# First mixers of a two-block transformer: order of decays, masks and their exponentials against splits of weights, and of a unit of v against the second decay sums

## What is computed

```python
def hgrn2(q, f_logit, i_in, lb):               # 4 heads of 64
    q = silu(q)
    f = lb + (1.0 - lb) * sigmoid(z)
    log_f = log(maximum(f, TINY))
    k = (1.0 - lb) * sigmoid(-z)
    v = i_in
    # in chunks: c = cumsum(log_f)
    #   o = (q * exp(c)) @ state + (sum_k q k exp(c_t - c_s), causal) @ v
    #   state = exp(c_last) * state + (k * exp(c_last - c)).T @ v

def forgetting_attention(q, k, v, f_logit, g_q, g_k):   # 8 heads of 64
    q = rms(q) * g_q; k = rms(k) * g_k
    dcum = cumsum(log_sigmoid(f_logit))
    logits = q @ k.T * scale + dcum_q - dcum_k          # causal softmax, @ v

for l in range(DEPTH):
    z = rms_norm(x, norm_mix[l]) @ w_in[l]
    (a_q, a_k, a_v, a_f, c_x, c_b, c_c, r_q, r_f, r_i, r_g) = split(z)
    y = concatenate([forgetting_attention(...), short_conv(...), hgrn2(...)])
    x = x + (rms(y per head) * gain, last part * silu(r_g)) @ w_out[l]
    x = x + (swiglu or the routed experts)(rms_norm(x))
# then the second block: three attentions and a squared-relu feed-forward, per layer
```

## Time and profile before

| | us |
|---|---|
| median of three runs | 2675.93 |
| lowest and highest | 2669.7, 2685.15 |
| the profiled execution, its own time | 2669.63 |
| its span | 2667.8 |
| TensorE busy | 2534.3 (95%) |
| VectorE busy | 1919.3 (72%) |
| ScalarE busy | 1489.4 (56%) |
| mean granted clock of TensorE | 0.979 |

### The profile page before, as it was taken

One profiled execution on the slowest core, in us unless ns is written; L12 is line 12 of the kernel. 1 busy time (PEld: TensorE's weight loads), 2 busy tenths in 40 slices (PEclk: granted clock), 3 DMA queues, 4 the chain that ended last, 5 costly groups with the idle time before them and its releaser, 6 DMA issues.

```text
span 2667.8 us, 38535 instructions
## 1 busy us (share of the span) xinstructions
PE 2534.3 (95%) x16700; PEld 2259.1 (85%) x16700; DVE 1919.3 (72%) x1702; ACT 1489.4 (56%) x1460; POOL 0.2 (0%) x4
## 2 busy tenths in 40 slices
PE   7989999988999999999999999899999999999998
PEld 6879999777787878787787877888999998899998
DVE  6666556665788888888888888746776575667655
ACT  5354345443676777676677767446544354465433
POOL 0000000000000000000000000000000000000000
PEclk9999999898999999999999999999999999999999
DMA  6225544221799989999998999432435443243452
GB/s 235 94 79 196 184 178 155 106 75 57 274 362 350 364 345 359 352 352 355 352 360 343 352 355 364 179 123 99 142 129 203 177 164 134 97 142 143 174 189 81
DMA packets 83451, 585.31 MB, mean 219 GB/s; under 512 B 9416, under 2 KB 11176, under 8 KB 12752
## 3 DMA queue, kind: packets, MB, share of 16 engines
q1 hardware_dynamic: 83280, 582.81, 58.8%
HBM read 581.72 MB, written 1.05 MB: 218 GB/s over the span
## 4 chain that ended last, share of the span: by engine, by line
PE 79%; DVE 12%; ACT 6%; issue 2%; DMA 1%; DVEq 0%; ACTq 0%
PE PS L1620 77%; DVE wlo L962 4%; ACT whi L526 3%; DMA raw<-in_wm 1%; PE PS L2096 1%; ACT pb L629 1%; ACT pt L643 1%; DVE hT L1011 1%; PE PS L1825 1%; DVE rstd L1003 1%; DVE pb L1130 0%; DVE stat L1118 0%; DVE pb L1112 0%; ACT hhi L553 0%; DVE hlo L978 0%
## 5 line engine op out<-in xcount | busy, mean ns | idle before, releaser
L962 DVE TENSOR_TENSOR wlo<-raw,whi 128x2048 fp32r<-128x2048 f32 x550 | 1258.1, 2290 | 409.1 <-ACT whi L526 399.4
L526 ACT ACTIVATE whi<-raw 128x2048 fp32r<-128x2048 f32 x550 | 1051.3, 1913 | 310.5 <-PE PS L1620 283.5
L1620 PE MATMUL PS<-hhi,whi 128*128 128x256 f32 x1984 | 573.4, 289 | 10.4 <-DVE wlo L962 3.8
L1620 PE MATMUL PS<-hlo,whi 128*128 128x256 f32 x1984 | 565.7, 285 | 0.0
L1620 PE MATMUL PS<-hhi,wlo 128*128 128x256 f32 x1984 | 565.5, 285 | 0.0
L1620 PEld LDWEIGHTS PS<-hhi,whi 128*128 128x128 f32 x1984 | 385.1, 194 | 25.4 <-issue 13.3
L1620 PEld LDWEIGHTS PS<-hlo,whi 128*128 128x128 f32 x1984 | 385.2, 194 | 0.2
L1620 PEld LDWEIGHTS PS<-hhi,wlo 128*128 128x128 f32 x1984 | 384.8, 194 | 0.0
L1620 PE MATMUL PS<-whi,xghi 128*128 128x512 f32 x896 | 360.5, 402 | 2.3 <-ACT pm L770 2.1
L1620 PE MATMUL PS<-wlo,xghi 128*128 128x512 f32 x896 | 355.7, 397 | 0.0
L1620 PE MATMUL PS<-whi,xglo 128*128 128x512 f32 x896 | 355.5, 397 | 0.0
(11 more groups left out here) (351 smaller groups left out, 3643.2 us busy)
## 6 DMA issues: line engine op xcount, KB each, us to landing
raw<-in_wm SPq DMA_DIRECT2D x336, 1024.0 KB, 5.5
raw<-in_ws SPq DMA_DIRECT2D x214, 1024.0 KB, 4.8
xT<-in_xT SPq DMA_DIRECT2D x4, 256.0 KB, 6.7
bsum<-in_bsum SPq DMA_DIRECT2D x1, 1024.0 KB
out_T<-hT SPq DMA_DIRECT2D x4, 256.0 KB, 2.5
lmask<-in_lmask SPq DMA_DIRECT2D x1, 512.0 KB
lbw<-in_lbw SPq DMA_DIRECT2D x1, 256.0 KB
tri<-in_tri SPq DMA_DIRECT2D x1, 256.0 KB
```

Of the source, the lines that this page charges most:

```text
L526: act.activation(whi[s % SPLIT][:], raw[s % RAW][:], ACT.Copy).then_inc(hi_ready, 1)
L962: dve.tensor_tensor(wlo[s % SPLIT][:], raw[s % RAW][:], whi[s % SPLIT][:].bitcast(F32), ALU.subtract).then_inc(lo_ready, 1)
L1620: return pe.matmul(out, a, b, start=start, stop=stop, skip_group_check=True)
```

## The change

In the lists of the three engines some entries change places; the instructions stay the same in kind and number. On VectorE the split ahead of L1212 is taken out there and the splits behind it keep their order and take other places: the splits are then unit 4 after L1212, unit 5 after `decayed(0)` and the bias, 6 after levels 0 to 2, 7 after levels 3 to 5, 8 after levels 6 and 7, 9 ahead of `decayed(1)`, 10 after `head_inverse` and levels 0 and 1. `head_inverse` comes ahead of levels 0 and 1 of the second half. On ScalarE the split of unit 5 with the copy of unit 3 comes after `cum_exp`, and the split of unit 9 with the copy of unit 7 ahead of the second `cum_exp`. On TensorE unit 7 comes ahead of `decay_sums(1)` and unit 8 ahead of levels 0 and 1 of the second half.

```diff
@@ first_mixer on ScalarE @@
                 out_of(6, flat(ri))
-                out_of(7, pair(qkT, 0))
                 after(rk_turned)
                 act.activation(flat(rk), PS[:, 4, :], ACT.Copy).then_inc(rk_ready, 1)
                 cum_exp()
+                out_of(7, pair(qkT, 0))
...
                 head_square(qkT[:], hT[:])
+                out_of(7, vtok[:, :, 0:UC], wide=NT)
                 cum_exp()
-                out_of(7, vtok[:, :, 0:UC], wide=NT)
                 head_root(5, 16, 1.0 / HD)
@@ first_mixer on VectorE @@
                 dve.tensor_tensor(flat(rq), flat(rq), flat(cy), ALU.mult)
-                drain()
                 after(f_logged, 2)
                 dve.tensor_tensor(lf[:], lf[:], lf2[:], ALU.add).then_inc(decays_ready, 1)
                 drain()
...
                 drain()
                 levels(0, (3, 4, 5))
+                drain()
                 after(decay_taken, 2)
...
                 step(dve.tensor_scalar(qs1[:], vec1(l, "qg"), HD ** -0.5, None, ALU.mult))
+                levels(0, (6, 7))
                 drain()
-                levels(0, (6, 7))
                 dve.wait_ge(decayed_ready, C.now(decayed_ready))
                 step(dve.tensor_copy(kx[:], ke[:, :, LEVELS - 1, :]))
+                drain()
                 decayed(1)
-                drain()
+                head_inverse(16)
                 levels(1, (0, 1))
-                head_inverse(16)
                 drain()
@@ first_mixer on TensorE @@
                 levels(0, (6, 7))
+                project(unit_tok, 7)
                 decay_sums(1)
-                project(unit_tok, 7)
                 head_sums(8, lambda t: selw[:, t, :], 16, hT, 5)
+                project(unit_tok, 6)
                 levels(1, (0, 1))
-                project(unit_tok, 6)
                 head_spread(8, lambda t: selT[:, t, :], 16, [4, 5])
```

## The result

The changed kernel takes 2657.89 us (median of five runs, 2656.56 to 2662.63), the kernel before 2675.93: ratio 0.9932, 95% interval 0.9909 to 0.9954. The forecast was 2665.4 us, in a range of 2651 to 2680. The gain is 18 us where the sum gave 10.5. The profiled execution took 2662.63 us (span 2660.8), the slowest of the five; that of before, 2669.63, was its fastest. So the pair of profiles differs by 7 us and the medians by 18, and the question was where the other 11 are.

What follows compares the result with a forecast made beforehand. TensorE, busy 95% of the span, was taken as the bound. Layer gains of 4.30 and 1.99 plus clock 3.19 and 5.82 made 15.3, less 4.8 gave 10.5 us: 2665.4 against the median 2675.93, range 2651 to 2680.

Steps and rivals of the forecast that it cites:

- Keys: TensorE ahead of turning the keys: the decay sum is ready earlier, so holes of 2.71 and 3.44 us go.
- The place of the first q's copy: ScalarE, copy moved behind the exponential: the exponential waits for TensorE either way, so it changes nothing.
- Split of unit 5 behind the masks: TensorE ahead of level 2: the 3.38 us hole shrinks to 0.34, gaining 3.04 in layer 0, none in layer 1.
- The unit of v ahead of the decay sums: TensorE ahead of the second decay sums: the unit covers the 1.89 us wait, gaining 1.89 in each layer.
- what is late next: TensorE ahead of the third head-norm spread: VectorE's queue makes a 3.84 us stall instead of 0.50, losing 3.34 per layer.
- The clock: TensorE's low clock in both mixers: 9.01 us could come back, less 4.8 for new stalls and logits.
- (a): Rival, chance 0.20: the clock stays high after the new stall and in the logits; all 15.3 us gained, 2660.6.
- (f): Rival, chance 0.10: only idle holes lower the clock, logits cost nothing, each new stall one short stretch; 12.1 us gained, 2663.8.
- (b): Rival, chance 0.15: the low clock stretches are long, four of 3.09 us; 2.9 us gained, 2673.0.
- (e): Rival, chance 0.05: second-half exponential serial, 7.0 us moving into each third-spread stall; slower, 2679.4, or 2685.6 with more low clock.
- (c): Rival, chance 0.06: unit 5 comes late since its split stands behind the multiplications; 6.5 us left, 2669.4.
- (d): Rival, chance 0.04: nothing shows, since another wait fills the holes ahead of the keys; 2676.

Runs made afterwards that it cites:

- copy_back: The changed kernel with the first q's copy and unit 5's split ahead of the keys' copy and exponential on ScalarE again; 2659.28 us, 0.9929 of the kernel before.
- unit8_back: The changed kernel with the second unit of v behind levels 0 and 1 again on TensorE; 2661.94 us, 0.9949 of the kernel before.
- before_again: The kernel before, unchanged, run and profiled once more; median 2677.18 us, ratio 1.0005, profiled execution 2676.22 us.
- late_only: The kernel before with only the second half of the change (units of v moved earlier, split and head_inverse moved); 2678.42 us, ratio 1.0013.
- early_only: The kernel before with only the first half: decay sum ahead of splits, splits up to unit 7 behind masks, first q's copy moved; 2657.80 us, ratio 0.9931.

## Why the prediction was right, and where its size was off

**Keys.** Right: the sum of the decays is ready at 38.83, TensorE is free at 40.07 and turns the keys at once; the holes of 2.71 and 3.44 us are gone. The place of the first q's copy: nothing, shown by copy_back.

**Split of unit 5 behind the masks.** Right for layer 0: the hole is 0.35 us, the split ends at 53.3 and unit 5 begins at 57.0, without a wait. It isn't the low clock over unit 4 that hides it: unit8_back has 0.35 at full clock. The step that failed is "a gain of 3.04 in layer 0, none in layer 1". It read the 0.34 us of layer 1 as the stage's own, while it was the low clock over logits and unit 4 that had filled a hole of 3.38. The hole stands there in two of the three profiles with this first half (before_again, late_only), and a low stretch behind it: level 2 to the next levels takes 8.9 us (490.13 to 499.04) against 6.59. So the gain of layer 1 was mis-sized: its mixer took 107.1 us in the profile that the sum was made from and 112.4 in the usual one, 5.3 more. With it the sum of 10.5 becomes 15.8; 15.0 is what the mixers of the usual and the changed profile differ by.

**The unit of v ahead of the decay sums, and what is late next.** Right in both: no wait there, and 3.77 and 3.78 us ahead of the third spread where 3.84 was worked out. The balance of this half is slightly negative at most: late_only is 3.5 us slower by the ratio and 1.4 between the medians. The head sums start at 83.26 where 81.4 was forecast; 1.5 us of that are the low clock over unit 4.

**The clock.** The charge was 4.8 us; it came to 6.0 in this pair of profiles. From the third spread to the end of unit 9 it is 12.0 and 12.4 us against 10.7 and 10.7 before, 1.3 and 1.7 more (1.6 was taken); logits and unit 4 lost 1.5 us in each layer, where half of 1.6 was taken. The mixers became 9.4 us shorter, against 10.5; these 1.2 us account for it. Half a stretch per layer for the logits is near what all profiles show: 7 of 14 layers have one. Of the Trainium skill's warning of idle gaps ("TensorE: Matmul & The Clock Gate", "Why this matters for your kernels"): the low stretches behind the stalls of 3.4 to 3.8 us agree. But gaps weren't the only thing it followed here: the low stretch over unit 4 came in 7 of 14 layers with no idle time of TensorE in the 12 us ahead of it (in the changed kernel the last is the wait of 1.52 us ahead of unit 3, until 34.27, and the stretch begins at 47.9).

**The base.** The forecast was made against 2675.93, the sum against a profile 6.3 us below that. That distance was carried as a constant of the run; 5.6 us lie between the mixers of the first profile and of the usual one, and the change removed them. So 2665.4 came within 8 us of the result with two mis-sized terms that partly cancel: the gain of layer 1 too small by 5.3, the price of the low clock by 1.2. What is left between 15.0 and 17.5 to 18 us wasn't located, and is smaller than what the rest scatters by from profile to profile: the same code from the last matmul of the experts with `xghi` to the end took 1004.7 to 1011.9 us in these profiles.

**The rivals.** (a) and (f) came nearest in time, (a) for the wrong reason, since the clock did fall at both places. (f) is refuted by the low stretches over unit 4 with no hole ahead. Of (b) the mechanism came in half, at a smaller price: the low stretches from the stall on are long, 6.8 and 10.2 us, but cost 1.3 and 1.7 us and not 3.09. (e) is refuted by the stall of 3.77 us, (c) by unit 5, (d) by the interval. The time fell by 0.68%, and "faster by over 0.5%" had 0.31, too little, for the same failed step.

## What to carry to other kernels

Where two passes over the same code show a hole of 3.4 us in one and 0.3 in the other, look at the clock of the engine ahead of it before calling the second free: a slow stretch fills a hole, and the next run may have the hole, with more slow stretches behind it. Take a second profile before the gain is sized, and look how far the time of a profiled execution lies from the median of its kernel. A step that feeds the busiest engine goes ahead of queued work that nobody awaits yet; and when work is moved behind a wait, count the queue of the engine that serves the next one, since the stall came out to 0.07 us of that count. Before both halves of such a change are kept, run each alone.

## What the runs showed of the hardware

The granted clock of TensorE fell to its lower level (0.50) with no idle time in the 12 us ahead, over a unit right behind 32 narrow matmuls of 8 columns that stand together (in two layers it fell before they had ended): for 3.4 us in both layers of the changed kernel, and in 7 of 14 profiled layers with this order, at 1.5 or 3.0 us each. It stayed at 1.00 in the six profiled layers in which the same 32 stood between wide matmuls, and in the two with 4 of them.

A hole of 1.89 us ahead of the second decay sums was followed by the low clock in five of six profiled layers (both of before_again and of early_only, layer 0 of the first profile), where the sums take 5.37 us in place of 3.6.

And an execution with a low stretch can be the faster one: the kernel before took 107.1 us for its second mixer with the low clock over logits and unit 4, which filled the hole ahead of level 2, and 112.4 us with the full clock there, the hole, and low stretches behind it. Why the low stretches behind it stayed away in the first isn't shown.
